# Gate chunks, the last gate projection and the late gate rows take other places in a GLA and DSA decoder step

## The chip, the cores and the metric

One core of a Trainium2 chip runs the whole step as one hand-scheduled program. The metric is device time in microseconds, from launch to end. Engines are named as in the profile: PE (TensorE) multiplies, DVE (VectorE) and ACT (ScalarE) work elementwise, POOL (GpSimd) and SP (SyncE) mostly issue DMAs. Each engine runs its own instruction list in order and meets the others only at semaphores.

## The reference

A two-layer decoder trunk is run once for a prompt of 256 tokens and for 8 samples of one token each (264 columns in all), with model width 1024. Layer 0 mixes tokens by gated linear attention (GLA), layer 1 by sparse attention over a selected set of keys (DSA); behind each comes a mixture of 64 experts.

```python
for i in range(DEPTH):
    sh1p, sc1p, gt1p, sh2p, sc2p, gt2p = ada_mod(c_prompt, w_ada[i], b_ada[i])   # silu(c) @ w + b, cut in six
    hp = modulate(xp, norm_mix[i], sh1p, sc1p)
    ...
    xp = xp + gt1p[:, None, :] * mp          # mp: gla_mixer (i = 0) or dsa_mixer (i = 1)
    xp = xp + gt2p[:, None, :] * moe_ffn(modulate(xp, norm_ffn[i], sh2p, sc2p), *mo)
# gla_mixer: q, k, v, r, g1 = split(h @ w_in); log_a = log_sigmoid(g1 @ w_g2 + b_g2) / 16
#   samples: S = exp(g) * S + k v^T;  o = q S
#   o = rms_norm(o) * silu(r);  return o @ w_out, S
```

The gate vectors of `ada_mod` have 6 x 1024 entries per layer. Of those, the mixer's input needs the first two (shift and scale); the third is needed when the mixer's output is added, the last three by the experts.

## The kernel before

All weights come through `ring`, four slots (`WS`) of three thirds, 3 MB each (3.15 million bytes). `plan` hands out slots in the order of use at build time, and each load waits for `slot_used` of its slot's last user. SP issues all loads in one order, so a load that waits holds up all behind it.

The matrix `w_ada` of a layer is cut in 8 chunks of 768 columns. For one chunk, `pe_ada_rows` (`L440`) makes 48 short matmuls into PSUM (the gate *rows*), ACT copies them to `mrow` (`act_ada`, `L513`), `pe_ada_fold` (`L451`) turns and adds them with 12 matmuls (the *fold*) and `dve_ada` (`L519`) adds the bias into `modT`, counted by the semaphore `mod_T`. Chunks 0 to 2 hold what the input of the GLA needs. `pe_late_rows` (`L538`), `act_late_rows` (`L550`), `pe_late_fold` (`L558`) and `dve_late` (`L568`) are the same for chunks 4 to 7 of layer 1, inside the DSA.

*Start of the GLA.* SP loads gate chunks 0 to 4, then the four chunks of `gla_w_in` with gate chunks 5, 6 and 7 between them, then `gla_w_out`. PE does gate chunks 0 to 4, then the low-rank gate product (`L737`), its second factor (`L741`), and then 24 projection products of 128 columns (`L757`, 16 matmuls each, six to a chunk); rows and folds of gate chunks 5 to 7 stand between them. Products 0 to 15 are q, k and v, which DVE evicts; 16 to 23 are the gate `r`, on which ACT applies Silu (`gate(m_)`) and POOL scales by the norm weights (`scale_gate`, four products at a time, `L1112`).

*End of the GLA.* From product 16 on, one step of `pe_gla_core` follows each product: transposes (`L788`), scores, state updates of the prompt (`dve_state`, `L1027`), the product inside a chunk (`pe_within`, `L841`) and the product with the running state (`pe_across`, `L850`). The eight samples go through `pe_outer` (k v^T, `L882`), `dve_sample` (the update, `L1053`) and `pe_sample_o` (q S, `L888`). `pe_turn_on` (`L897`) turns the normalised output and `dve_mix` (`L1045`) multiplies by the gate. POOL loads the sample states (`load_state`) and stores them. Then `pe_out_proj` (`L910`) follows.

*End of the DSA.* The prompt's attention runs as a pipeline over 8 steps `it`: `logits` on PE, mask and maximum on DVE, exponentials on ACT, division on DVE (`L2378`), `turn_probs` on PE (`L2116`), a copy on ACT (`L2492`), `mix_values` on PE (`L2127`). The samples follow: `turn_rows` (`L2168`) turns the gathered key rows, and `L2180` is the first product of their logits. POOL gathers the key and value rows meanwhile (`L1956`). Each engine's order is written out by hand.

## Time and profile before

| | |
|---|---|
| median of 3 runs | 1698.36 us (1695.97 to 1700.70) |
| the profiled execution | 1698.2 us |
| its span, first to last instruction | 1696.4 us |
| PE busy / DVE / ACT / POOL | 95% / 42% / 26% / 9% |
| mean granted PE clock | 0.977 of full |
| HBM read, over the span | 337 GB/s |
| GLA, from `L737` to the output projection | 57 to 243 us |
| experts of layer 0 | about 300 to 850 us |
| DSA, until its output projection begins | about 870 to 1065 us |

The profile counts time from the first instruction. "Busy" of PE is the share in which a matmul is under way; the ends of matmuls are modelled. A clock of 1.0 is 2.4 GHz and 0.5 is 1.2 GHz. `x48` behind a row is the number of instructions joined in it.

### The profile page before, as it was taken

What the parts mean: (1) busy time and instruction counts of PE and PEld (TensorE: products, weight loads), DVE (VectorE), ACT (ScalarE), POOL (GpSimd) and SP (SyncE); (2) the same over time, 40 slices, a digit from 0 to 9 for tenths busy, and PEclk for the clock granted to TensorE, in tenths of its full rate; (3) what the DMA queues carried; (4) which work ended last, traced back from release to release, by engine and by line L of the source; (5) the groups of instructions that cost most, each with busy time, mean ns of one, the idle gap of its engine ahead of it and who ended that gap; (6) DMA issues with size and microseconds to landing.
All of it is one profiled execution on the core that took longest, in us unless ns stands there. A gap on an engine that the chain in (4) does not pass through costs nothing. (4 is left out here: it accounts for less than half of the span.)

```text
span 1696.4 us, 30818 instructions
## 1 busy us (share of the span) xinstructions
PE 1613.6 (95%) x11730; PEld 953.5 (56%) x11730; DVE 707.2 (42%) x1918; ACT 447.6 (26%) x997; POOL 146.9 (9%) x208
## 2 busy tenths in 40 slices
PE   6999899999999999999989988989999999999997
PEld 4678576555555455555466755755555555545554
DVE  2133536463333333334246952276433333333334
ACT  2211221222222232222232133122222222223223
POOL 0001300000000000000020052000000000000000
PEclk9899899999999999999999988899999999999999
DMA  9975648799999999999584344459999999999990
GB/s 358 362 262 170 257 149 323 311 385 404 417 416 416 417 409 416 412 417 415 196 311 145 130 160 128 156 188 372 398 410 417 416 417 414 413 417 415 413 366 26
DMA packets 139032, 552.38 MB, mean 326 GB/s; under 512 B 19407, under 2 KB 36637, under 8 KB 104662
## 3 DMA queue, kind: packets, MB, share of 16 engines
q1 hardware_dynamic: 120562, 513.82, 76.3%
q0 software_dynamic: 15392, 34.66, 5.7%
q10 hardware_dynamic: 3012, 3.00, 0.5%
q8 instruction: 45, 0.74, 0.2%
q14 instruction: 21, 0.17, 0.0%
HBM read 562.74 MB, written 8.60 MB: 337 GB/s over the span
## 5 line engine op out<-in xcount | busy, mean ns | idle before, releaser
L1445 PE MATMUL PS<-ring,arena 128*64 128x256 f32 x4288 | 490.7, 382 | 2.6 <-ACT arena L1775 1.5
L1445 PEld LDWEIGHTS PS<-ring,arena 128*64 128x64 f32 x4288 | 304.7, 137 | 182.2 <-issue 41.2
L1469 PE MATMUL PS<-ring,arena 128*64 128x512 f32 x1072 | 259.6, 605 | 1.4 <-ACT arena L1760 1.4
L1408 PE MATMUL PS<-arena 128*128 128x512 bf16 (+1 forms) x796 | 197.4, 384 | 0.0
L1677 DVE TENSOR_TENSOR arena<-arena,PS 128x128 f32<-128x128 f32 x134 | 38.6, 288 | 371.1 <-ACT arena L1758 365.1
L1661 DVE TENSOR_SCALAR arena<-arena 128x512 bf16<-128x512 f32 x130 | 62.8, 483 | 256.5 <-ACT arena L1769 256.5
L1768 ACT COPY arena<-PS 64x512 f32<-64x512 f32 x134 | 77.5, 578 | 302.2 <-PE PS L1469 302.2
L1469 PEld LDWEIGHTS PS<-ring,arena 128*64 128x64 f32 x1072 | 65.1, 136 | 120.4 <-issue 104.0
L1758 ACT ACTIVATE arena<-PS 128x128 f32<-128x128 f32 x134 | 37.2, 278 | 326.5 <-PE PS L1445 326.5
L1408 PEld LDWEIGHTS PS<-arena 128*128 128x128 bf16 (+1 forms) x796 | 69.6, 99 | 91.9 <-issue 27.7
L1399 PEld LDWEIGHTS PS<-cst,arena 128*128 128x128 f32 x552 | 72.1, 195 | 80.2 <-issue 78.3
L1788 POOL COPY arena<-arena 128x1 int32 (+1 forms) x71 | 14.5, 204 | 1139.1 <-PE PS L1399 934.4
L1399 PE MATMUL PS<-cst,arena 128*128 128x128 f32 x552 | 98.0, 300 | 2.0 <-ACT arena L1775 1.4
L1663 DVE SCALAR_TENSOR_TENSOR arena<-arena 128x512 f32<-128x512 f32 x130 | 97.7, 751 | 4.6
L1667 DVE TENSOR_TENSOR arena<-arena 128x512 bf16<-128x512 f32 x130 | 90.0, 692 | 4.5
L757 PE MATMUL PS<-hT,ring 128*128 128x264 f32 x384 | 90.3, 394 | 0.3 <-DVE modT L519 0.3
L1775 ACT COPY arena<-PS 128x512 f32<-128x512 f32 x135 | 79.5, 589 | 28.9 <-PE PS L1399 27.3
L757 PEld LDWEIGHTS PS<-hT,ring 128*128 128x128 f32 x384 | 73.2, 193 | 15.4 <-issue 2.8
L1769 ACT COPY arena<-PS 64x512 f32<-64x512 f32 x134 | 77.9, 582 | 1.6
L1790 POOL DMA_INDIRECT arena<-h_rows,arena x71 | 72.7, 1024 | 61.6 <-POOL arena L1788 58.3
L1760 ACT COPY arena<-PS 128x128 f32<-128x128 f32 x134 | 35.7, 266 | 138.3 <-PE PS L1457 138.3
L910 PE MATMUL PS<-shT,ring 128*128 128x264 f32 x256 | 64.0, 409 | 0.9 <-DVE shT L2420 0.6
(512 smaller groups left out, 1552.0 us busy)
## 6 DMA issues: line engine op xcount, KB each, us to landing
ring<-in_moe_w_gate SPq DMA_DIRECT2D x134, 1024.0 KB, 7.7
ring<-in_moe_w_up SPq DMA_DIRECT2D x134, 1024.0 KB, 10.0
ring<-in_moe_w_down SPq DMA_DIRECT2D x134, 1024.0 KB, 15.6
ring<-in_w_ada SPq DMA_DIRECT2D x32, 1152.0 KB
ring<-in_w_ada SPq DMA_DIRECT2D x16, 768.0 KB
ring<-in_gla_w_in SPq DMA_DIRECT2D x8, 1152.0 KB
ring<-in_dsa_w_in SPq DMA_DIRECT2D x6, 1024.0 KB
arena<-in_state_gla POOLq DMA_DIRECT2D x8, 512.0 KB, 8.6
```

The costliest lines, as they stand in the source:

```text
L757: m = pe.matmul(PS[:, b, 0:TOK], w8_[:, k, (m_ % 6) * P:(m_ % 6 + 1) * P], hT[:, k, 0:TOK], start=(k == 0), stop=(k == KT - 1))
L910: m = pe.matmul(PS[:, 4 + k % 4, 0:TOK], w3[:, kk, (k % 2) * P:(k % 2 + 1) * P], src[:, kk, :], start=(kk == 0), stop=(kk == KT - 1))
L1399: ins_ = pe.transpose(PS[:, 6, k * P:(k + 1) * P], xv[:, 4 * half + k, :], K["ident"])
L1408: ins_ = pe.matmul(PS[:, c, :], oh[:, T * P:(T + 1) * P], y[:, 512 * j:512 * j + 512], start=False, stop=True, skip_group_check=True)
L1445: m = pe.matmul(PS[64 * half:64 * half + 64, 5, 0:256].rearrange("p (g n) -> p g n", g=2), rows[:, k, CAP * b:CAP * b + CAP], gu[:, :, k, ...
L1469: m = pe.matmul(PS[64 * j:64 * j + 64, 7, :], hTt[b][:, kk * CAP:(kk + 1) * CAP], ring[:, s, 2, kk * D + 512 * j:kk * D + 512 * j + 512], ...
L1663: dve.scalar_tensor_tensor(out=ysb[par][:, q], in0=ysb[par][:, q], scalar=wv[:, par:par + 1], in1=yw[:, 0, q], op0=ALU.mult, op1=ALU.subtr ...
L1667: dve.tensor_tensor(yw[:, 2, q], ysb[par][:, q], yw[:, 1, q], ALU.subtract).then_inc(M(l, "split"), 1)
L1768: act.copy(ysb[par][q, 0:512], PS[0:CAP, 7, :])
L1769: act.copy(ysb[par][q, 512:D], PS[CAP:P, 7, :]).then_inc(M(l, "ysb"), 1)
L1775: act.copy(xgT[into][:, 4 * half:4 * half + 4, :].rearrange("p k c -> p (k c)"), bank(6)).then_inc(M(l, "xgT"), 1)
L1790: pool.indirect_dma_start(out=xg[into], out_offset=None, in_=hrow_d[l], in_offset=IndirectOffsetOnAxis(ap=gi[:, into:into + 1], axis=0), b ...
```

## The change

In the GLA, gate chunks 3 and 4 are loaded behind the first chunk of `gla_w_in` and done between projection products (rows of chunk 3 after product 3, of chunk 4 after 5, of chunk 5 after 9; 6 and 7 as before). The last projection product is placed behind `pe_across(3)` and the outer products of samples 1 and 2; ACT applies its Silu after the squares of the second half, POOL scales after it has issued the load of state 4, and the turns and multiplies of the output take another order among the samples. In the DSA, the rows of gate chunk 6 go from step 8 of the pipeline to its end, into other banks (0 and 4), their fold goes behind two groups of `turn_rows`, and `turn_rows` uses its four banks in another rotation.

```diff
--- before.py
+++ after.py
@@ -310,12 +310,11 @@
-        it_ada = [plan(5), None]
+        it_ada = [plan(3), None]
         it_gla = []
-        for _ in range(3):
+        for n_ada in (2, 2, 1, 0):
             it_gla += plan(1)
-            it_ada[0] += plan(1)
-        it_gla += plan(1)
+            it_ada[0] += plan(n_ada)
         it_gout = plan(2)
@@ -725,8 +724,7 @@
                 load_wide(item, w_in, 768 * i)
-                if i < 3:
-                    sp_ada(0, [5 + i])
+                sp_ada(0, ((3, 4), (5, 6), (7,), ())[i])
             for i, item in enumerate(it_gout):
@@ -740,7 +738,7 @@
             m.then_inc(S("gla_pe"), 1)
-            pe.wait_ge(S("mod_T"), 5)
+            pe.wait_ge(S("mod_T"), 3)
             for m_ in range(24):
@@ -761,16 +759,17 @@
                     pe.sem_inc(S(f"slot_used{item[0]}"), 1)
-                    if m_ == 5:
-                        pe.wait_ge(S("softplus"), 1)
-                        pe_ada_rows(0, 5, 4)
-                    if m_ == 11:
-                        pe_ada_rows(0, 6, 4)
-                if m_ == 13:
-                    pe_ada_fold(0, 6, 4)
-                    pe_ada_rows(0, 7, 4)
+                if m_ == 3:
+                    pe.wait_ge(S("softplus"), 1)
+                    pe_ada_rows(0, 3, 4)
+                if m_ in (5, 11, 13):
+                    i = (m_ + 1) // 2 if m_ > 5 else 4
+                    pe_ada_fold(0, i - 1, 4)
+                    pe_ada_rows(0, i, 4)
                 if m_ == 7:
-                    pe_ada_fold(0, 5, 4)
+                    pe_ada_fold(0, 4, 4)
+                if m_ == 9:
+                    pe_ada_rows(0, 5, 4)
                 if m_ == 15:
@@ -818,10 +817,10 @@
                 pe_outer(0)
-            elif step == 7:
                 pe.wait_ge(S("state"), 4)
+                pe_across(3)
                 pe_outer(1)
-                pe_across(3)
+                pe_outer(2)
@@ -852,19 +851,20 @@
         def pe_gla_rest():
-            pe_outer(2)
+            pe_outer(3)
             pe.wait_ge(S("proj_act"), 8)
             pe_sample_o(0)
+            pe_turn_on(1, 0, 2, 2)
             pe_sample_o(1)
-            pe_outer(3)
+            pe_outer(4)
+            pe_turn_on(1, 1, 3, 2)
             pe_turn_on(0, 1, 1, 1)
-            pe_turn_on(1, 0, 2, 2)
-            pe_turn_on(1, 1, 3, 2)
             pe_sample_o(2)
-            for b in range(4, DEC):
+            pe_sample_o(3)
+            for b in range(5, DEC):
                 pe_outer(b)
@@ -942,10 +942,8 @@
                 ins_.then_inc(S("proj_dve"), 1)
-                if m_ == 9:
-                    dve_ada(0, [5], 4)
-                if m_ == 15:
-                    dve_ada(0, [6], 4)
+                if m_ in (6, 8, 12, 15):
+                    dve_ada(0, [{6: 3, 8: 4, 12: 5, 15: 6}[m_]], 4)
                 if m_ == 5:
@@ -998,12 +996,13 @@
             dve_on(1)
-            dve_mix(0, 0, 1)
             dve_sample(3)
-            dve_mix(0, 1, 1)
-            dve_mix(1, 0, 2)
-            dve_mix(1, 1, 3)
-            for b in range(4, DEC):
+            dve_mix(0, 0, 1, 1)
+            dve_mix(1, 0, 2, 2)
+            dve_sample(4)
+            dve_mix(1, 1, 3, 3)
+            dve_mix(0, 1, 1, 4)
+            for b in range(5, DEC):
                 dve_sample(b)
@@ -1038,10 +1037,10 @@
-        def dve_mix(T, half, b):
+        def dve_mix(T, half, b, turned):
             dve.wait_ge(S("r_scaled"), half + 1)
-            dve.wait_ge(S("on_turned"), 2 * T + half + 1)
+            dve.wait_ge(S("on_turned"), turned)
             dve.tensor_tensor(oT[:, 4 * half:4 * half + 4, T * P:(T + 1) * P], bank(b).rearrange("p (j t) -> p j t", t=P),
@@ -1065,14 +1064,15 @@
             act.activation(eg, Lg[:, :, SEQ:TOK], ACT.Exp, scale=-1 / 16)
+            act_ada(0, [3], 4)
             act.wait_ge(S("gla_dve"), GD["dL"] + 1)
             act.activation(ke, dL, ACT.Exp, scale=1 / 16).then_inc(S("exps"), 1)
-            act_ada(0, [5], 4)
+            act_ada(0, [4], 4)
             act.wait_ge(S("gla_dve"), GD["dE"] + 1)
             act.activation(cL, cL, ACT.Exp, scale=-1 / 16).then_inc(S("exps"), 1)
-            act_ada(0, [6, 7], 4)
+            act_ada(0, [5, 6, 7], 4)
             def gate(m_):
@@ -1081,7 +1081,6 @@
                     gate(22)
-                    gate(23)
                     act.wait_ge(S("on_ready"), 1)
@@ -1093,6 +1092,8 @@
                     act.activation(oms[:, 0:1], oms[:, 0:1], ACT.Sqrt, bias=K["eps"], scale=1 / GDV).then_inc(S("o_rms"), 1)
+                if T == 1:
+                    gate(23)
                 if T > 0:
@@ -1115,10 +1116,10 @@
                 load_state(b)
-            scale_gate(1)
             pool.wait_ge(S("state"), 4)
             load_state(4)
+            scale_gate(1)
             pool.dma_start(outs["gla_p"][0, 0].rearrange("h d v -> d h v"), Sst[1]).then_inc(S("out_pool"), 16)
@@ -2143,16 +2144,14 @@
                     logits(it)
-                if it == 8:
-                    pe.wait_ge(S("logit_sb"), 8)
-                    pe_late_rows(6, 0)
                 if it == 2:
                     mix_values(it - 3)
-            pe_late_fold(6, 5, 0)
+            pe.wait_ge(S("logit_sb"), 8)
+            pe_late_rows(6, 0, 4)
             dve_at(pe, "oht")
@@ -2165,14 +2164,16 @@
                     for h in range(2):
-                        m = pe.transpose(PS[:, 4 + b % 4, (2 * Pq + h) * P:(2 * Pq + h + 1) * P], Kg[:, h, b, P * Pq:P * Pq + P], K["ident"])
+                        m = pe.transpose(PS[:, 4 + (b + 1) % 4, (2 * Pq + h) * P:(2 * Pq + h + 1) * P], Kg[:, h, b, P * Pq:P * Pq + P], K["ident"])
                 m.then_inc(S("krow_T"), 1)
             turn_rows(0)
-            pe.wait_ge(S("mod_T"), 15)
             turn_rows(1)
+            pe_late_fold(6, 4, 256)
             dve_at(pe, "Qs")
             for b in range(DEC):
+                if b == 1:
+                    pe.wait_ge(S("mod_T"), 15)
                 if b + 2 < DEC:
@@ -2394,7 +2395,7 @@
             ins_.then_inc(S("dsa_dve"), 1)
-            dve_late(6, 5, 0)
+            dve_late(6, 4, 256)
             pe_at(dve, "slogit")
@@ -2500,12 +2501,11 @@
                     exps(it)
-                elif it == 8:
-                    act_late_rows(6, 0)
                 probs_out(it - 2)
                         act.dma_start(dst, src).then_inc(S("kv_out"), 16)
+            act_late_rows(6, 0, 4)
             mixed_out(1)
@@ -2513,7 +2513,7 @@
                     act.wait_ge(S("klogit"), b - 3)
-                act.copy(KTs[b % 4][:, :, 0:256], bank(4 + b % 4).rearrange("p (q n) -> p q n", q=2))
+                act.copy(KTs[b % 4][:, :, 0:256], bank(4 + (b + 1) % 4).rearrange("p (q n) -> p q n", q=2))
                 act.copy(KTs[b % 4][:, :, 256], kT[:, :, SEQ + b]).then_inc(S("krow_sb"), 1)
@@ -2566,7 +2566,7 @@
             sp_setup()
-            sp_ada(0, range(5))
+            sp_ada(0, range(3))
             sp_gla()
@@ -2590,7 +2590,7 @@
             pe_ada_fold(0, 0)
-            pe_ada(0, range(1, 5))
+            pe_ada(0, range(1, 3))
             pe_gla()
@@ -2614,7 +2614,6 @@
             dve_modulate(0, 0)
-            dve_ada(0, [3, 4])
             dve_gla()
@@ -2632,7 +2631,7 @@
             act_norm(0, norm_sq, 3, between=lambda: act_ada(0, [0]))
-            act_ada(0, range(1, 5))
+            act_ada(0, range(1, 3))
             act_gla()
             act_shift(1, 0, 1)
```

## Rows read from the trace of the kernel before

**Rows 1.** The page: PE busy and granted clock in 40 slices, and a DMA queue.

```profile
PE   6999899999999999999989988989999999999997
...
PEclk9899899999999999999999988899999999999999
...
q8 instruction: 45, 0.74, 0.2%
```

**Rows 2.** One window of the expert stage: busy us of each engine, clock, DMA.

```profile
760.00:780.00 20.00, 19.95 (x151) 10.52 (x148) 5.96 (x13) 5.74 (x13) 2.40 (x4) 1.00 1.02 416
```

**Rows 3.** Timeline, start of the GLA: start, us, engine, line, operation, idle before.

```profile
43.99 5.35 PE L440 MATMUL PS<-ring,cT 128*32 128x256 f32 x48 [1.06 <-DMA ring<-in_w_ada]
44.12 2.67 DVE L649 TENSOR_SCALAR hT<-hT,modA,modT 128x256 f32<-128x256 f32 x8
...
57.22 3.73 PE L737 MATMUL PS<-hT,arena 128*16 128x264 f32 x16
...
63.51 16.86 PE L757 MATMUL PS<-hT,ring 128*128 128x264 f32 x67
```

**Rows 4.** Window at the start of the GLA; the last three: PEclk, DMA share, GB/s.

```profile
44.50:49.90 5.40, 4.84 (x48) 1.90 (x40) 2.29 (x8) 0.50 (x1) 0.00 (x0) 0.50 1.03 402
```

**Rows 5.** Timeline of PE in the projection of the GLA.

```profile
87.13 2.80 PE L440 MATMUL PS<-ring,cT 128*32 128x256 f32 x48 [0.30 <-PE PS L757]
89.86 7.39 PE L757 MATMUL PS<-hT,ring 128*128 128x264 f32 x32
97.08 1.40 PE L451 MATMUL PS<-cst,mrow 128*128 128x9 f32 x12
98.34 14.49 PE L757 MATMUL PS<-hT,ring 128*128 128x264 f32 x64
```

**Rows 6.** Timeline, end of the GLA.

```profile
180.37 1.66 DVE L1027 SCALAR_TENSOR_TENSOR arena<-arena,PS 128x256 f32<-128x256 f32 x4 [3.79 <-PE PS L850]
...
185.23 1.13 PE L882 MATMUL PS<-arena 8*128 8x256 f32 x8
185.61 3.19 POOL L1112 TENSOR_SCALAR arena<-arena,vT 128x528 f32<-128x528 f32 x2 [2.75 <-ACT arena L1078]
...
186.29 1.94 PE L850 MATMUL PS<-arena 128*64 128x256 f32 x8
...
202.07 2.08 PE L882 MATMUL PS<-arena 8*128 8x256 f32 x8
...
204.19 1.66 DVE L1053 SCALAR_TENSOR_TENSOR arena<-arena,eg,PS 128x256 f32<-128x256 f32 x4 [1.33 <-PE PS L882]
```

**Rows 7.** Window over the last samples and the output projection of the GLA.

```profile
200.00:220.00 20.00, 17.13 (x79) 10.73 (x76) 7.14 (x21) 1.21 (x5) 2.29 (x4) 0.66 0.47 184
```

**Rows 8.** The page: DMA issues, KB each, median us from issue to landing.

```profile
arena<-in_state_gla POOLq DMA_DIRECT2D x8, 512.0 KB, 8.6
```

**Rows 9.** Timeline of the DSA, with the block of gate rows of chunk 4 first.

```profile
943.87 2.80 PE L538 MATMUL PS<-ring,cT 128*32 128x256 f32 x48
...
1022.04 2.49 PE L538 MATMUL PS<-ring,cT 128*32 128x256 f32 x36
...
1022.37 1.23 DVE L2378 TENSOR_TENSOR arena<-arena 128x1024 f32<-128x1024 f32 x1
...
1024.27 0.99 ACT L2492 COPY arena<-PS 128x1024 f32<-128x1024 f32 x1
...
1025.35 2.58 PE L538 MATMUL PS<-ring,cT 128*32 128x256 f32 x12 [0.82 <-issue]
...
1029.56 0.94 POOL L1956 DMA_INDIRECT ring<-in_cache_v,arena  x1 [0.30 <-issue]
...
1031.31 0.59 ACT L550 COPY hT<-PS 128x512 f32<-128x512 f32 x1 [6.05 <-remote]
...
1042.39 1.13 PE L2180 MATMUL PS<-arena 128*128 128x257 f32 x4
```

**Rows 10.** Window behind the block of chunk 6 in the DSA.

```profile
1031.50:1036.50 5.00, 4.92 (x30) 4.29 (x31) 0.00 (x0) 1.78 (x3) 0.00 (x0) 0.51 0.84 279
```

## The prediction

> **What bounds the kernel now.** I read the slices of the page first [rows 1]: TensorE (PE) is at nine tenths in nearly every one, and its clock stands below the top level in only a few, near the start, near slices 23 to 25 and at the end. The windows of the long expert stages come second [rows 2]: in 20 us the matmul engine is busy 19.95 us and the DMA engines are full as well. The change touches no line there, so such a stage only starts earlier or later. What can move is the three stretches whose order is rewritten: the start of the linear attention (GLA), its end, and the end of the sparse attention (DSA). There I read the timeline, in order of time, asking at each step which wait ended last.
>
> At the start of the GLA the PE does the gate rows (`L440`, one 3 MB `w_ada` chunk each) as the chunks land; chunk 3 landed at 43.99 [rows 3]. While it works on chunks 3 and 4, `hT` is long ready (VectorE, DVE, makes it from 44.12 on), and the low-rank gate product (`L737`) starts only at 57.22, the first projection product (`L757`) at 63.51. From there to 137 us PE has almost no gap [rows 5]. At the end of the GLA the sample states alternate between PE (outer product, `L882`) and DVE (update, `L1053`, 1.66 us each) [rows 6]. At the end of the DSA, gate rows of chunk 6 (`L538`) stand in the middle of the softmax pipeline, and they are strange [rows 9].
>
> **The change part by part.** Sums are made against the profiled execution (span 1696.4 us, its time 1698.2 us with 1.8 us around the span), which is 0.16 us under the median of 1698.36.
>
> *Part A, gate chunks 3 and 4 go behind the first projection weights.* The SP queue is served in order, so the first projection chunk takes the place of chunk 3 and lands at 43.99 instead; chunks 3 and 4 follow 7.8 us apart, at about 52 and 60, long before their new places after the fourth and sixth product. Each weight chunk after that keeps its place or comes later by one slot use: chunk 5 now waits for the slot of the first projection chunk (free near 78), is needed near 98 and takes 7.8 us (3.15 MB at the 402 GB/s of [rows 4]): hidden. Chunk 7 waits for the slot that the product of `m_` 11 frees and is needed after a fold (1.26), rows (3.0), two products (7.2) and a fold, 12.8 us later, against some 10: 2.8 us of cover. If that cover were gone each further us is paid in full.
> PE would start `L737` when the first eighth of `hT` is out, 44.12 + 0.41 = 44.5. In the profile 6.29 us pass from `L737` to `L757` (57.22 to 63.51) [rows 3] at the upper clock level (2.4 GHz). But from 44.5 to 49.9 the granted clock is 0.50, the lower level of 1.2 GHz [rows 4], after PE had sat idle waiting for chunks. 5.4 us at half rate put 2.7 us on top: first projection product at 44.5 + 6.3 + 2.7 = 53.5, 10.0 us earlier than before. Inside the projection two chunks are added: rows 89.86 - 87.13 plus a 0.3 gap in front = 3.0, fold 98.34 - 97.08 = 1.26 [rows 5], twice = 8.6. ACT and DVE have their small copies and adds to do one step later than PE needs them in no case; the ACT copy of chunk 3 needs 1 us after 70, its fold comes at 78. The sum is -1.4 us. Bounds: with no low clock on the way the start is at 50.8, -4.1; with 3.4 us more of it (the slow stretch of [rows 4] lasting 8.8 instead of 5.4), +0.3. I take -1.4, as the same gaps stand in front.
>
> *Part B, the end of the GLA.* State 3 is ready at 180.37 + 1.66 = 182.0 [rows 6], so `pe_across(3)` can run from 182.2 to 184.1 where it now waits behind the last projection product (which ends before 185.2) and ends at 188.2. The outer products of samples 1 and 2 (1.06 each) follow, 186.2; the last projection product then runs 186.2 to 189.9, sample 3's outer product to 191.0. ScalarE (ACT) does the squares of the second half from 184.1 instead of 188.3, DVE has `on_ready` 2 at about 190.5 instead of 193.4. The last gate (`gate(23)`) comes at 190.4 and GpSimd (POOL)'s scaling, 3.19 us, ends at 193.7 instead of 188.8; the first multiply that needs it waits for sample 4 and comes at 196.8, so it is covered by 3 us. Behind that scaling on POOL stand the store of the prompt state and the sample stores, 4 us later; the last store is issued after sample 7 in either order. The load of state 4 moves the other way, ahead of the scaling, from 188.8 to 184.1; with the page's 8.6 us to landing [rows 8] it is there at 192.7, before sample 4's turn at 195.1; by the same 8.6 us it lands at 197.4 now. Following DVE: sample 3 at 191.1, 4 at 195.1, 5 at 198.3, 6 at 200.1, 7 at 201.9 instead of 204.19. That is -2.3, and up to -2.6 at the last product. The clock takes part of it back: from 200.1 on it is low (mean 0.66 over the window 200 to 220) [rows 7], and an outer product then takes 2.08 instead of 1.13 [rows 6]. Two on the path cost 1.0 more, so -1.3. Bounds -4.3 (the low stretch, which now reaches into the output projection, ends one step earlier and gives 1.7 back) and +1.0 (it begins one step earlier).
> What a page says stands by itself here. The row shows 8.6 us for a state load [rows 8]. The Trainium skill (DMA: Bandwidth & Descriptors, "Issuing engines are not separate DMA queues") says that transfers of all issuing engines interleave on the same 16 DMA engines; a 3 MB ring load issued at the same time would by that rule put some 8 us on state 4 and 5 us on the sum. As the ring load of that moment waits for the slot of the product that is moved to 189.9, it would by the same rule do less harm than now.
>
> *Part C, the last gate rows of the DSA.* The two blocks of `L538` at 943.87 and 962.97 take 2.80 us for 48 matmuls. The third starts at 1022.04, does 36 of them in 2.5 us, trickles through 12 more from 1025.35, and only at 1031.31 does ACT get the result: 9.3 us instead of 2.8 [rows 9]. PE goes on then at the lower clock level (0.51 in the window 1031.5 to 1036.5) [rows 10], and the first sample logit product (`L2180`) is at 1042.39 [rows 9]. All that DVE and ACT owe to it was done by 1026, so PE alone is late.
> The change does these rows after the last `mix_values` instead, their fold behind two transposes. With durations at the upper level: turn 6 when DVE's division (1022.37 + 1.23) is done, 1023.7 to 1024.8; mix 5 after ACT's copy (1024.27 + 0.99), 1025.4 to 1026.5; turn 7 to 1027.5; mix 6 to 1028.6; mix 7 after another ACT copy of 1.0, 1028.9 to 1030.0; rows to 1032.8; four transposes 0.63 and two groups of 0.55 to 1034.6; ACT's two copies (1.0) and then `mixed_out` (1.0) and the one-hot copy (0.6) end at 1035.6; fold 1.4, to 1036.0; three groups start again and the first logit product is at 1036.6. That is 1042.4 - 1036.6 = -5.8 us. The wait for `mod_T` 15, now at `b == 1`, asks for a DVE add of 0.21 us that is done a transpose group earlier; no cost. The slot of chunk 6 is freed 1.5 us later than now; its next load is needed at 1065, with some 20 us to spare. Bounds: if the block is as slow in its new place, the rows end at 1039.2 and what follows until the first logit product (3.8 us) runs at the lower level, 1046.1, so +3.7; if the kernel before were usually free of it, its own chain would reach that product at about 1034.0, so +2.6.
>
> Sum: -1.4 - 1.3 - 5.8 = -8.5, so 1689.7 against the profiled execution and 1689.9 against the median. I say 1690.
>
> **The rivals.** *First, the stall belongs to its time or its place in the instruction stream, not to the rows.* Samples' value rows are being gathered by POOL until 1030.5 (1029.56 + 0.94), the stall ends 0.8 us later [rows 9]. Then PE stands still from about 1026 to 1031.3 in any order: mix 6 and 7, rows, transposes and fold come after it, first logit product at 1039.8 with 2 us at half rate already in it, C is -2.6, in all 1693.1. For it: no twin of the block stalled, so the code of the rows alone does not do it. Against: the first 36 matmuls of the block ran at full pace with the same gathers under way.
> The page lists 45 instruction packets on q8 [rows 1]. The Trainium skill (Runtime: NRT & Kernel Launch, "Instruction fetch mechanics") has an engine's instructions fetched in order in blocks of 256; by that rule a late block would hit whatever instruction stands at that count, and the result would be this rival's 1693.1. The trace neither shows nor excludes that.
> *Second, on the other side: the stall follows the rows.* A burst of 96 short PE instructions beside the gathers stalls, and now it stands alone on the path, with `mixed_out` and the one-hot copy of ACT queued behind the copy that waits for it. C is +3.7. It decides the sign from the point where A and B give less than 3.7 together: with their 2.7 it is 1699.2, and with B at its upper bound 1701.5. For it: the rows' weights and the gathers are the same, and the gathers end (1030.5) just when the moved rows run. Against: two of three blocks were fast.
> *Third, the profiled stall is not in the usual execution.* Then C is +2.6, since before the rows filled waits of PE that now stay open, and the sum is -0.1: 1698.2. For it: a single trace. Against: the profiled execution is within 0.2 us of the median, so its 9 us can hardly be extra.
>
> **How the numbers follow.** Forecast 0.50 (own range 1686 to 1693), first rival 0.22, second 0.12, third 0.16. The range goes from 1684 (A or B well towards their lower bounds) to 1702, which takes in the third and the second rival. A measurement of this kernel can tell 0.3%, 5.1 us: faster means under 1693.3. The forecast gives 0.46 of it, the first rival 0.12: 0.58. Slower (over 1703.4) needs the second rival with A and B failing: 0.06. The rest, 0.36, is no change.
>
> **What would show it.** `L737` at about 44.5 and the first `L757` at 51 to 54; the first `L788` about 1.4 earlier; `pe_across(3)` ahead of the last `L757`; sample 7 on DVE 2 to 4 us earlier in absolute time; the block of `L538` after the last `L2127` in 2.8 us, first `L2180` 5.8 us after what the shift of parts A and B alone gives. Wrong would be: PE idle on a ring load inside the projection; the low clock stretching over the first projection products; a block of `L538` of over 5 us; or a gain in a stretch that is lost before the experts start.

## The result and the profile after

The changed kernel takes 1692.32 us (median of 15 runs, 1686.33 to 1695.54), the kernel before 1700.7 us in the same session (15 runs, 1694.61 to 1704.33). The ratio is 0.9949 [0.9938, 0.9961], which is 8.7 us less, between 6.6 and 10.5. The profiled execution of after took 1688.6 us with a span of 1686.8, so it lies 3.7 us under its median, as the profiled execution of before lies 2.5 us under the 1700.7. The differences by stage below are between these two executions (1698.2 and 1688.6, 9.6 us), and how far two executions can be trusted for them is said at the end of this section.

The page of after, the granted clock in 40 slices and the state loads, beside [rows 1] and [rows 8] (the slices of PE busy and the 45 packets of q8 are the same as before):

```profile
PEclk9999898999999999999999989999999999999999
...
arena<-in_state_gla POOLq DMA_DIRECT2D x8, 512.0 KB, 7.4
```

The slices look alike. The clock has a 9 for an 8 in slice 2 and in slices 25 and 26 (the late part of the DSA), and an 8 for a 9 in slice 7. Everything else must be read in the three stretches.

*Start of the GLA.* Timeline of after, and two windows (busy us of PE, PEld, DVE, ACT, POOL, then PEclk, DMA share, GB/s), beside [rows 3] and [rows 4]:

```profile
44.35 2.67 DVE L648 TENSOR_SCALAR hT<-hT,modA,modT 128x256 f32<-128x256 f32 x8
...
44.90 6.11 PE L735 MATMUL PS<-hT,arena 128*16 128x264 f32 x16 [1.74 <-DVE hT L648]
...
53.57 12.73 PE L755 MATMUL PS<-hT,ring 128*128 128x264 f32 x56
```

```profile
44.50:51.50 7.00, 6.11 (x16) 2.02 (x16) 2.90 (x9) 0.00 (x0) 0.00 (x0) 0.62 1.03 401
135.00:138.60 3.60, 3.60 (x11) 2.75 (x10) 0.00 (x0) 0.00 (x0) 0.00 (x0) 0.53 0.00 0
```

The first projection product is at 53.57 where it was at 63.51, 9.94 us earlier. The window from 44.5 has a mean clock of 0.62. The last fold inside the projection starts 2.97 us earlier (132.29 for 135.26). Two chunks of 4.3 us were added, which would leave 1.3; the other 1.6 come from a low stretch that before has over its first projection products and after hasn't (0.63 in before, 1.00 in after over 64 to 68 us). In before:

```profile
64.00:68.00 4.00, 4.00 (x13) 3.15 (x12) 0.00 (x0) 3.96 (x7) 0.00 (x0) 0.63 1.03 400
```

Then a stretch at the low level over the last product of after (0.53 from 135.0 to 138.6) takes 1.7 back, and the first transpose of the core is 1.28 us ahead:

```profile
139.43 1.91 PE L787 MATMUL PS<-cst,arena 128*128 128x128 f32 x16
```

against this of before:

```profile
140.71 1.91 PE L788 MATMUL PS<-cst,arena 128*128 128x128 f32 x16
```

*End of the GLA.* Timeline of after, beside [rows 6]:

```profile
180.79 1.94 PE L849 MATMUL PS<-arena 128*64 128x256 f32 x8 [0.75 <-DVE arena L1026]
...
188.95 3.19 POOL L1113 TENSOR_SCALAR arena<-arena,vT 128x528 f32<-128x528 f32 x2 [4.89 <-ACT arena L1078]
...
193.65 1.66 DVE L1052 SCALAR_TENSOR_TENSOR arena<-arena,eg,PS 128x256 f32<-128x256 f32 x4 [0.86 <-PE PS L882]
...
198.97 1.15 PE L882 MATMUL PS<-arena 8*128 8x256 f32 x8
...
200.16 1.66 DVE L1052 SCALAR_TENSOR_TENSOR arena<-arena,eg,PS 128x256 f32<-128x256 f32 x4 [0.18 <-PE PS L882]
...
206.96 5.41 PE L910 MATMUL PS<-shT,ring 128*128 128x264 f32 x16 [0.38 <-DVE shT L1012]
```

`pe_across(3)` stands at 180.79, the last sample's update at 200.16 instead of 204.19, and the output projection begins at 206.96, where before has 209.71. The low stretch of [rows 7] starts at 200.0 here too (0.50 in 200 to 204, where before has 0.51). The load of state 4 is issued at 183.30 instead of 188.80.

*End of the DSA.* Timeline of after, beside [rows 9]:

```profile
1020.94 1.09 PE L2117 MATMUL PS<-cst,arena 128*128 128x128 f32 x8 [1.53 <-issue]
...
1022.60 2.03 PE L2128 MATMUL PS<-arena 128*64 128x128 f32 x16 [0.57 <-issue]
...
1024.56 1.77 PE L2117 MATMUL PS<-cst,arena 128*128 128x128 f32 x8
...
1026.26 2.32 PE L2128 MATMUL PS<-arena 128*64 128x128 f32 x32
...
1026.85 0.95 POOL L1957 DMA_INDIRECT ring<-in_cache_v,arena  x1 [0.30 <-issue]
...
1028.51 2.80 PE L537 MATMUL PS<-ring,cT 128*32 128x256 f32 x48
1031.37 0.59 ACT L549 COPY hT<-PS 128x512 f32<-128x512 f32 x1 [3.99 <-PE PS L537]
...
1034.55 1.03 PE L2181 MATMUL PS<-arena 128*128 128x257 f32 x4
```

The 48 matmuls are one piece of 2.80 us, just behind POOL's last gather issue (1027.80). The first sample logit product is at 1034.55 instead of 1042.39: 7.84 us earlier, of which 2.7 had been there since the GLA. The window that answers [rows 10] is at the full clock:

```profile
1031.50:1036.50 5.00, 5.00 (x39) 4.78 (x40) 0.21 (x1) 4.42 (x11) 0.00 (x0) 1.00 0.82 266
```

The idle times of 1.53 and 0.57 us in these rows are no part of a stall: DVE's division ends at 1020.88 (1019.65 + 1.23), ACT's copy at 1022.55, and PE goes on within 0.1 us of each.

By stage, after minus before, same PE instruction: core of the GLA -1.28, output projection -2.75, first expert of layer 0 (305.99 to 305.05) -0.94 and later in that stage -2.6, last of the DSA before the rows -2.7, sample logits -7.84, output projection of the DSA (1064.97 to 1055.93) -9.04, end -9.6.

*What one pair of executions is worth.* The experiments below left more profiles, on several chips. Seven of them have the GLA exactly as in before. Their first projection product stands at 65.06 to 67.04 us (before: 63.51); the gate product `L737` in front of it takes 5.1 to 5.4 us in them (3.73 in before), so a low stretch falls earlier. Their output projection begins at 211.80 to 213.78 (before: 209.71). The four profiles with parts A and B (`after`, `after2`, `ab`, `ab_vhold`) have that projection at 204.90 to 210.09. The means, 212.4 with the profiled before among them and 208.0, are 4.4 us apart, where the one pair says 2.75. So differences of 1 to 3 us between two single profiles are within what executions of the same code differ by, in the GLA at least.

### The profile page after: what moved, and what is told of

Same layout as the page of the kernel before. It is cut to its first block and busy times, and to the rows that moved or that the text cites. A ratio compares the mean times of both kernels' runs of the same rounds, so it can differ in the third digit from the quotient of the medians.

```text
span 1686.8 us, 30821 instructions
## 1 busy us (share of the span) xinstructions
PE 1608.3 (95%) x11730; PEld 950.1 (56%) x11730; DVE 707.3 (42%) x1918; ACT 449.7 (27%) x999; POOL 147.5 (9%) x208
## 5 line engine op out<-in xcount | busy, mean ns | idle before, releaser
L1791 POOL DMA_INDIRECT arena<-h_rows,arena x71 | 72.7, 1024 | 61.6 <-POOL arena L1789 58.3
```

Source lines behind the costliest of these rows:

```text
L1791: pool.indirect_dma_start(out=xg[into], out_offset=None, in_=hrow_d[l], in_offset=IndirectOffsetOnAxis(ap=gi[:, into:into + 1], axis=0), b ...
```

## Experiments

Two views were open. *The theory*: the slow block is a matter of PE beside POOL's gathers, and the change takes it off the path, while A and B give only what their own stretches show. *The rivals*: the three of the prediction, and one more, that the parts don't add. The experiments ran on three chips, each with its own runs of the kernel before: chip 2 has before at 1688.56 and, later, at 1688.34, chip 3 at 1699.87 (one run), chip 4 at 1700.13. The chip of the result (before 1700.7) is called chip 1; the record doesn't name it, so it may be chip 3 or chip 4.

A distance inside the DSA is used for all: from the first one-hot product (`L2088` of before) to the first sample logit product (`L2180`). What shifts both drops out. It is 66.8 us in the profiled before and 61.6 in after. The kernel before was not profiled on chip 2; for it stand `a_only`, `b_only` and `ab`, whose DSA is that of before.

### Each part alone (chip 2)

`a_only`, the start of the GLA as in after, the rest as before:

```diff
-        it_ada = [plan(5), None]
+        it_ada = [plan(3), None]
...
-                    sp_ada(0, [5 + i])
+                sp_ada(0, ((3, 4), (5, 6), (7,), ())[i])
...
+                if m_ == 3:
+                    pe.wait_ge(S("softplus"), 1)
+                    pe_ada_rows(0, 3, 4)
```

> Only part A (gate chunks 3 and 4 behind the first projection weights) on top of the kernel before. My sum: the first projection product at 53.5, the first transposes of the core (140.71 before) 1.3 us earlier, in all 1.3 us or 0.08% faster. A theory in which the gain of the start is given back to the clock before the experts begin: first transposes earlier, but the route stage at the old time, no change.

`b_only`, the end of the GLA alone:

```diff
-            elif step == 7:
                 pe.wait_ge(S("state"), 4)
+                pe_across(3)
                 pe_outer(1)
-                pe_across(3)
+                pe_outer(2)
```

> Only part B (order at the end of the linear attention). My sum: output projection 1.3 to 1.5 us earlier than the 209.71 of before, 0.08% faster. Rival: the clock's low stretch around 200 takes it all, output projection earlier by under 0.5 us.

`c_only`, the order of the DSA alone:

```diff
-                if it == 8:
-                    pe.wait_ge(S("logit_sb"), 8)
-                    pe_late_rows(6, 0)
...
+            pe.wait_ge(S("logit_sb"), 8)
+            pe_late_rows(6, 0, 4)
```

> Only part C (late gate rows of chunk 6 at the end of the softmax pipeline). If the slow block of the profile of before is real in timed runs: 5.1 us faster (0.30%), block in 2.8 us, first sample logit product 5.1 us earlier. If it is only in the profiled execution: 2 to 3 us slower in the timed runs. If slowness follows the rows: the block takes 9 us here too and the kernel is 3 to 4 us slower.

Measured: A alone 1684.54 us, 0.9970 [0.9959, 0.9982], so -5.1 (expected -1.3). B alone 1686.41, 0.9983 [0.9974, 0.9991], so -2.9 (expected 0.08%, some -1.4). C alone 1692.50, 1.0024 [1.0012, 1.0036], so **+4.1** (expected -5.1 with the slow block, 2 to 3 us slower without it, 3 to 4 slower with the block as slow in its new place; the block took 2.8 us, so the second case, and more than its price). In none of the six profiles from this chip is the block slow. The block in the profile of `a_only`, in the old order:

```profile
1017.21 2.80 PE L537 MATMUL PS<-ring,cT 128*32 128x256 f32 x48
1020.31 0.58 ACT L549 COPY hT<-PS 128x512 f32<-128x512 f32 x1
1020.34 1.06 PE L2114 MATMUL PS<-cst,arena 128*128 128x128 f32 x8 [0.33 <-PE PS L537]
```

In one piece, ACT at once behind it; the distance is 57.0 us here (57.6 in `b_only`, 57.1 in `ab`), 9.2 to 9.8 shorter than in the profiled before of chip 1, and the kernel before is 12 us faster on this chip. So most of the difference between the chips is in this one stretch.

### The gathers held back (chips 2 and 4)

`vhold` keeps the second half of POOL's value gathers behind the gate rows of chunk 6, everything else as before. `vhold2` is the same kernel under another name on another chip:

```diff
                     if name == "vg_in" and h:
+                        pool.wait_ge(S("late_rows"), 3)
```

> The kernel before, but GpSimd starts the second half of the value gathers only when the gate rows of chunk 6 are finished. If the slow block (9.3 us from its first matmul to the copy that waits for it) comes from the gathers beside it: block in 2.8 us, first sample logit product near 1034 to 1035 instead of 1042.4. If it comes from the PE instruction stream (count of instructions, dense block): still 9 us.

`vhold` took 1688.07 us (one run) beside 1688.56: nothing to win where the block is fast anyway. It had to be run where the block is slow, together with a profile of the kernel before there, `before_p`.

> The kernel before, unchanged, for a profile on this chip beside the others. In the earlier calls the kernel before took 1688.6 us on one chip (where no variant had the slow block of gate rows) and 1699.9 on another (where two variants had it). Theory: the slow block is a matter of the chip, not of the kernel alone. Then the time here is near 1689 with a block of 2.8 us, or near 1699 with one of 8 to 9.5 us, and nothing between. Rival: the block varies from execution to execution on one chip.

`before_p` took 1701.37 us. Its timeline on chip 4:

```profile
1026.00 2.56 PE L538 MATMUL PS<-ring,cT 128*32 128x256 f32 x41
...
1029.39 1.35 PE L538 MATMUL PS<-ring,cT 128*32 128x256 f32 x7 [0.83 <-issue]
...
1033.50 0.95 POOL L1956 DMA_INDIRECT ring<-in_cache_v,arena  x1 [0.30 <-issue]
...
1035.58 1.94 PE L2116 MATMUL PS<-cst,arena 128*128 128x128 f32 x8 [4.83 <-remote]
```

The picture of [rows 9] again: 41 of the 48 at full pace, the others in pieces, and PE goes on (at the low level, 1.94 where 1.06 is usual) 1.1 us after the last gather was issued (1034.45). The distance is 66.4 us. One thing more is in these rows. All 48 matmuls are on record by 1030.7 here and by 1027.9 in [rows 9], but ACT, which only waits for their semaphore, starts at 1035.31 and at 1031.31. So the slow block is a trickle of matmuls and behind it, for 4.6 and 3.4 us, a result that is not announced. The trace can't tell whether these matmuls ended late (their ends are modelled) or only their semaphore came late.

> The kernel before, with the second half of the value gathers held until the gate rows of chunk 6 are done. If this chip has the slow block (kernel before near 1699) and the gathers cause it: block in 2.8 us, 7 to 9 us faster. If it has the slow block and the gathers are innocent: block still 9 us, same time. If this chip has no slow block: same time as before within 1 us.

Measured: 1699.19 us, 0.9997 [0.9979, 1.0014], where 7 to 9 us less had been expected if the gathers were to blame: the interval leaves room for 3.6 us of gain, not for 7. Its timeline on chip 4, PE and the gathers that were held:

```profile
1030.93 2.80 PE L538 MATMUL PS<-ring,cT 128*32 128x256 f32 x48
...
1034.06 1.06 PE L2118 MATMUL PS<-cst,arena 128*128 128x128 f32 x8 [0.33 <-PE PS L538]
```

```profile
1034.53 0.99 POOL L1958 DMA_INDIRECT ring<-in_cache_v,arena  x1 [10.89 <-PE PS L538]
...
1043.43 0.95 POOL L1958 DMA_INDIRECT ring<-in_cache_v,arena  x1 [0.30 <-issue]
```

```profile
1039.09 1.15 PE L2129 MATMUL PS<-arena 128*64 128x128 f32 x16 [0.79 <-issue]
1040.17 1.51 PE L558 MATMUL PS<-cst,hT 128*128 128x9 f32 x12
1041.64 0.55 PE L2161 MATMUL PS<-cst,arena 128*128 128x128 f32 x3
1042.35 0.27 PE L2161 MATMUL PS<-cst,arena 128*128 128x128 f32 x1 [0.16 <-issue]
1043.06 0.55 PE L2170 MATMUL PS<-cst,ring 128*128 128x128 f32 x3 [0.44 <-issue]
1043.78 0.27 PE L2170 MATMUL PS<-cst,ring 128*128 128x128 f32 x1 [0.17 <-issue]
```

```profile
1046.00 1.01 ACT L2498 COPY shT<-PS 128x1024 f32<-128x1024 f32 x1 [6.96 <-remote]
1046.12 0.21 DVE L568 TENSOR_TENSOR modT<-PS,bT 128x54 f32<-128x54 f32 x1 [6.35 <-remote]
```

This is the run that decides between the first two rivals. The rows are fast now that nothing is gathered beside them, and *other* instructions, transposes that have nothing to do with the rows, come in threes and ones about 0.7 us apart as long as the held gathers are under way. And here too results are announced late: ACT waits for the last `mix_values` (on record until 1040.24), DVE for the fold (until 1041.68), and both start at 1046.0 to 1046.1, 1.6 us behind the last issue (1044.38). In `vhold`, the same kernel on chip 2, the same copy starts at 1031.19, 0.04 us behind its matmuls. The stall moved with the gathers, not with the rows. It isn't DVE's work either: DVE is idle from 1039.8 to 1046.1 here.

In these single profiles the hold does buy something here: from the rows to the first sample logit product it is 17.6 us in `vhold2`, 20.4 in before and 19.8 in `before_p`. But the rows begin late in this execution, 49.7 us behind the first one-hot product instead of 46.5. PE stood for 1.47 us at 1010.4, beside gathers of the first half, and a stretch at the low clock followed (0.70 in 1012 to 1016). This execution took 1703.57 us, 4.4 above the median of its kernel, so the loss need not be usual.

### Another place for the rows, another place in the stream (chip 3)

`rows9` puts the rows one pipeline step later, `shift80b` puts 20 tiny matmuls, whose result nobody reads, in front of the one-hot products, so that every later PE instruction has 80 more before it:

```diff
-                if it == 8:
+                if it == 9:
                     pe.wait_ge(S("logit_sb"), 8)
                     pe_late_rows(6, 0)
```

```diff
+            for _ in range(20):
+                pe.matmul(PS[0:8, 7, 504:512], K["ident"][:, 0:8], cst[:, 0:8], start=True, stop=True, skip_group_check=True)
```

> The kernel before with the gate rows of chunk 6 one pipeline step later (it 9 instead of 8, on PE and on ACT). If the slowness belongs to the rows: 9 us again. If it belongs to the time (1024 to 1031, beside the gathers): the block starts at 1025 to 1026 and is hit for the rest of that time, 5 to 6 us. If it belongs to the place in the instruction stream (about 67 instructions behind a fetch): a dense block that starts 48 matmul instructions later has less or none of it, 2.8 us.

> The kernel before with 20 tiny matmuls (80 PE instructions) put ahead of the wait for the one-hot rows at 975, which moves all later PE instructions by 80 against the blocks of 256 in which they are fetched. If the block of gate rows is slow because a fetch comes due inside it: it is fast here (2.8 us) and something else may be slow. If it is slow because of the gathers or of itself: 9 us again at the same time. The 20 matmuls themselves cost about 1 us.

Measured, one run each beside 1699.87 of before: 1697.96 and 1703.12 us, no difference that single runs can show. Both blocks are slow, 6.0 us from the first matmul to ACT's copy in `rows9` (5 to 6 expected if the slowness belongs to the time, 9 if to the rows, 2.8 if to the place in the stream) and 5.7 in `shift80b` (9 or 2.8 expected). In `shift80b`:

```profile
1033.64 1.49 PE L538 MATMUL PS<-ring,cT 128*32 128x256 f32 x20
...
1034.76 1.24 POOL L1956 DMA_INDIRECT ring<-in_cache_v,arena  x1 [0.30 <-issue]
...
1035.98 0.59 PE L538 MATMUL PS<-ring,cT 128*32 128x256 f32 x2 [0.85 <-issue]
...
1037.42 1.89 PE L538 MATMUL PS<-ring,cT 128*32 128x256 f32 x26 [0.84 <-issue]
```

The last gather is issued by 1036.0; until 1037.4 PE does two matmuls, then 26 in a row. In `rows9` the last gather is issued by 1034.25, the last 11 matmuls start at 1035.02. The end of the stall keeps to the end of the gathers (0.8 to 1.4 us behind it) in four executions of three kernels, wherever the rows stand, and 80 instructions in front don't move it away.

### The change again, and with the held gathers (chip 4)

`after2` is the changed kernel; `ab_vhold` has parts A and B, the old order of the rows, and the gathers held as in `vhold`.

> The kernel with the whole change, beside the others on one chip. If this chip has no slow block: part C costs 4 us there and A and B give 8, so 4 us faster (0.24%). If it has: 9 to 12 us faster, with ab_vhold another 4 us ahead of it.

> Parts A and B of the change, with part C left out and the gathers held as in vhold2 instead. If parts A and B give 8 us, as a_only and b_only sum to on the chip where they ran (0.30% and 0.17%): 8 us faster without the slow block, 15 to 17 with it. By the shifts of my profile of after (2.7 us at the output projection): 3 us faster without it, 10 to 12 with it.

Measured: `after2` 1689.90 us, 0.9940 [0.9920, 0.9960], so -10.2; its block is fast and just behind the last issue (1031.17), and its distance 61.6 us as in after. That is the 9 to 12 us expected for a chip with the slow block. `ab_vhold` 1694.21, 0.9970 [0.9955, 0.9985], so -5.1, where 10 to 17 had been expected for such a chip, and 4.3 us behind `after2` instead of 4 ahead. Since the hold alone brought no gain that the runs show, these 5.1 us are an indication of what A and B give on this chip. Its distance, 64.0, is shorter than the 67.3 of `vhold2`; the 3.3 us lie ahead of the rows, at the stop of 1010.4 described above (rows 46.4 us behind the one-hot product here), and from the rows on both take 17.6.

### C alone again, and A with B (chip 2)

`c_only2` is `c_only` again; `ab` is both edits of the GLA and nothing in the DSA (the two diffs above together).

> Part C alone, repeated: the gate rows, their copies and the gate-sum fold of chunk 6 stand late in the expert choice's order, parts A and B as before. Theory (the PE's instruction issue is slow beside POOL's issue of the value gathers, on some chips only): where the kernel before takes about 1700 us and its block of 48 one-column matmuls takes over 4 us, this kernel's block takes about 2.8 us and behind the last gather issue, and the time is 5 us less than before, about 1695; first one-hot product to first sample logit product about 61.6 us. Where the kernel before takes about 1689 and its block 2.4 to 2.8 us, the time is 3 to 4 us more than before, about 1692.5, that distance about 60.1 us. Rival (part C costs on every chip, and parts A and B gave all of the gain): 3 to 4 us more than before also where the kernel before takes 1700.

> Parts A and B together, without C: gate chunks 3 and 4 behind the first projection's weights, the last gate chunk behind the last state product, and the order of the rows in the expert choice as before. Theory: their gain does not depend on the gathers: 3 to 8 us less than before on any chip (2.7 us by the shift alone, the rest by where the low-clock stretches fall). Where the kernel before takes about 1700 that is about 1694 to 1697, above the changed kernel's 1690 to 1692; where it takes about 1689 it is about 1681 to 1684, and about 3 to 4 us under what the changed kernel takes there. Rival (the three parts don't add): within 1 us of the kernel before.

Both ran where before takes 1688.34 us. `c_only2`: 1692.38, 1.0017 [1.0005, 1.0030], so +2.9, the sign of `c_only` confirmed, and the distance is the 60.1 expected. Part C alone was never run on a chip with the slow block. `ab`: 1684.18, 0.9974 [0.9964, 0.9984], so -4.4, within the 3 to 8 expected. It is less than the 8.0 that A and B alone add up to, and no better than A alone. PE in `c_only2`, and then in `ab`:

```profile
1023.62 1.12 PE L2127 MATMUL PS<-arena 128*64 128x128 f32 x16 [0.67 <-ACT shT L2496]
1026.28 1.09 PE L2116 MATMUL PS<-cst,arena 128*128 128x128 f32 x8 [1.54 <-DVE arena L2378]
1027.93 1.61 PE L2127 MATMUL PS<-arena 128*64 128x128 f32 x16 [0.56 <-ACT arena L2492]
...
1031.37 2.32 PE L2127 MATMUL PS<-arena 128*64 128x128 f32 x32
1033.62 2.80 PE L538 MATMUL PS<-ring,cT 128*32 128x256 f32 x48
```

```profile
1018.52 1.12 PE L2128 MATMUL PS<-arena 128*64 128x128 f32 x16 [0.67 <-ACT shT L2497]
1019.57 2.80 PE L537 MATMUL PS<-ring,cT 128*32 128x256 f32 x48
1022.70 1.06 PE L2117 MATMUL PS<-cst,arena 128*128 128x128 f32 x8 [0.34 <-PE PS L537]
1023.70 1.15 PE L2128 MATMUL PS<-arena 128*64 128x128 f32 x16
```

Here is the price of part C. From the first row of each to the end of the last `mix_values` and the rows together it takes 12.8 us in the new order (1023.62 to 1036.42), 9.6 in the old one (1018.52 to 1028.12). The rows in their old place fill the wait for DVE's division and for ACT's copy, 1.54 and 0.56 us idle in the new order, and a stretch at the low clock follows those waits (1.61 and 1.97 where 1.15 and 1.10 are usual). The same two waits, 1.53 and 0.57 us, are in after. The distances are 60.1 against 57.1 us.

## Why the prediction was right, and where it wasn't

The forecast of 1690.0 lies 2.3 us under the 1692.3 measured, and the forecast gain of 8.5 (8.4 from the median) meets the 8.7 of the same session and, within its interval, the 10.2 of chip 4. The three parts are right in kind. That their sizes fit to tenths is in part luck, as the first two points say. (The clock's slices are 9 at the end of [rows 1], where the prediction reads a lower level; nothing rests on that.) Step by step:

- **Part A's start held, its agreement at 139 us is luck.** Predicted: first product at 53.5 with a low stretch on the way, core 1.4 earlier; 53.57 and 1.28. None of the feared ring waits came up: no gap of the projection is put down to a DMA. But two low stretches that I had no step for cancel there: that of before at 64 to 68 us, which after is rid of (1.6 us gained), and that of after at 135 (1.7 lost). The first could be read from [rows 3], where a matmul takes 0.25 us (16.86 for 67) against 0.23 in [rows 5] (7.39 for 32). As a gain of the whole kernel on chip 2 the term is too small: -5.1 instead of -1.4, the point outside its own bound of -4.1, though the interval, -6.9 to -3.0, takes that in.
- **Part B's order of events held, to a few tenths in this pair of profiles.** With A's 1.4 taken off, the prediction has `pe_across(3)` at 180.8, POOL's scaling ending at 192.3, sample 4 at 193.7 and sample 7 at 200.5; the trace has 180.79, 192.14, 193.65 and 200.16. The output projection was to come 2.7 earlier, and comes 2.75. The profiles that share code differ by more than that, though, and their means put A and B together at 4.4 us at the output projection, not 2.7. State 4 was in time: its load took 5.1 us in after, where the next ring load is issued only at 188.54, and 7.9 in before, where it is issued at 188.80, 3.6 us behind a ring load of 3 MB (stores run beside it as well). The Trainium skill's statement that all issuing engines' transfers interleave on the same DMA engines (DMA: Bandwidth & Descriptors, "Issuing engines are not separate DMA queues") agrees with that in direction; the 8 us that the prediction drew from it are more than the 2.8 seen. That the new order does less harm than the old one is as the prediction had it. Alone, on chip 2, B gave -2.9 instead of -1.3.
- **Part C's size was right on the chip of the prediction and its sign wrong on another.** The logits came 5.1 us earlier than by the shift of A and B, against 5.8 predicted. A low stretch over `mix` 5 and `turn` 7 (2.03 and 1.77 us in the rows above), which the durations "at the upper level" left out, puts the rows 1.2 us behind the sum, and the way from their end to the first logit product, 3.2 us instead of 3.8, gives about half of it back. On chip 2 the same edit costs 2.9 to 4.1 us. That is the third rival with its +2.6, and the argument against it (the profiled execution agrees with the median, so it must be usual) could speak only for one chip: the slow block is usual there, stands in every profile of chips 3 and 4 that has the rows inside the pipeline and nothing held, and is absent on chip 2.
- **The first rival was nearer on the cause, the forecast on the consequence.** The stall belongs to the time of the gathers, as `vhold2` shows, not to the rows, so the second rival falls. But the first rival's price, -2.6, assumed that PE does nothing until 1031.3 in any order. In after the steps from `turn` 6 to the rows ran from 1020.9 to 1031.3, beside the gathers for most of that, and lost nothing to the stall; in `after2` the last `mix_values` stopped half way for 1.52 us, again with ACT's copy ahead of it released late ("remote"). The densest block stood behind the last issue in both. So gathers alone don't make the stall, and why so little was lost there isn't shown. That rival also carried the Trainium skill's description of instructions fetched in order in blocks (Runtime: NRT & Kernel Launch, "Instruction fetch mechanics"); q8 has 45 packets in before and after alike, 80 instructions in front didn't free the block, and the DMA view of the stalled stretches (1024 to 1032 in before, 1028 to 1036 in `before_p`, 1030 to 1036 in `rows9`, 1034 to 1038 in `shift80b`) has no packet on q8 at all (in `vhold2`, 1038 to 1046, there is one). So in four of these profiles none is seen on its way while PE stood, and nothing here speaks for this form of the rival.
- **The parts don't add**, and the sum took it that they do: -5.1, -2.9 and +4.1 alone, -4.4 for the first two together. One thought is that what a shift of 1 to 3 us is worth at the end hangs on which instructions the low-clock stretches then fall on. That they move is seen in windows over the end of the states and the start of the first expert stage on chip 2, first in `vhold` (there the GLA is that of before), then in `a_only`:

```profile
296.00:304.00 8.00, 7.70 (x19) 4.60 (x18) 4.46 (x8) 0.00 (x0) 0.00 (x0) 0.58 0.91 371
```

```profile
296.00:304.00 8.00, 6.56 (x34) 2.71 (x32) 0.00 (x0) 0.98 (x2) 0.18 (x1) 1.00 0.24 83
```

The same 8 us are at 0.58 in the one and at the full clock in the other. Over 290 to 320 us, however, the mean is 0.89 in both, and 0.89 to 0.91 in all fourteen profiles, so the stretch has moved and is not shorter. At the core of the GLA `a_only` is 1.6 us ahead of `vhold` (139.01 and 140.58), at its output projection 3.9 (207.93 and 211.80), at the first one-hot product of the DSA 5.6 (971.91 and 977.46). These are single executions, and `ab`, with the same start as `a_only`, has its core at 141.43. Whether the clock or the spread between executions makes the parts fail to add is not shown.

What stays open: why PE's matmuls and the semaphores behind them are late beside the gathers on some chips and not on chip 2; what A and B together, or C alone, give on a chip where they are; and the changed kernel itself on chip 2. There its time would by the sums be about that of before (-4.4 for A and B, +2.9 to +4.1 for C, an estimate that adds parts), and `ab` the better kernel; on chips 1 and 4 the changed kernel is the fastest measured.

## What to carry to other kernels

A stall put down to "issue" in one profile can belong to the chip: look whether its distance is the same on a second one before an order is rewritten around it, for the rewrite costs where the stall is absent (here +3 to +4 us, against about -5 where it is present, as read from a pair of profiles). Follow what the stall ends with (here the last gather's issue, in three kernels) rather than the instruction it happens to hit, and look when the waiting engines are released, not only when the matmuls are on record. Where PE is dense, work out each shift by rows, but take the rows from several executions: here the same code stood 4 to 5 us apart at the output projection of the GLA, and a term of 1 to 2 us came out as 3 to 5.

## What was not expected of the hardware

- One kernel on one core takes 1688.5 us on one chip (medians of 1688.56 and 1688.34) and 1700 us on at least two others; some 9.5 of the 12 us lie between the one-hot product and the sample logits, 57 against 66.5 us.
- One block of 48 gate-row matmuls took 2.8 us on chip 2 and 9.3 us on chips 1 and 4 until their result could be used, in the same DSA code, with POOL's indirect gathers, one issue every 1.25 us, beside them on either. The DMA engines were two thirds idle meanwhile: the window 1026 to 1036 of `before_p` has a DMA share of 0.32 and 92 GB/s.

```profile
1026.00:1036.00 10.00, 4.26 (x52) 2.14 (x51) 7.40 (x13) 3.63 (x11) 6.65 (x6) 0.81 0.32 92
```

- Holding the gathers back moved the stall to other PE instructions, with no change of the time that the runs show, 0.9997 [0.9979, 1.0014].
- On the chips with the stall, a semaphore that a matmul of PE raises was seen by ACT, DVE and PE up to 5.8 us after the matmul's recorded end (`vhold2`, 1040.24 to 1046.00), and 0.04 us after it in the same kernel on chip 2. The ends of matmuls are modelled, so it may be the matmuls themselves that ended late.
